# Recurrence of a streaming encoder layer: the chain of one tile placed among the levels of the next tile

## What is computed

```python
def wkv_scan(r, decay, k, v, kk, a, state0):
    def step(S, inp):
        r_t, w_t, k_t, v_t, kk_t, a_t = inp
        sa = jnp.einsum('bhij,bhj->bhi', S, -kk_t)
        S = (S * w_t[:, :, None, :] + sa[..., None] * (kk_t * a_t)[:, :, None, :]
             + v_t[..., None] * k_t[:, :, None, :])
        y = jnp.einsum('bhij,bhj->bhi', S, r_t)
        return S, y
...
    kk = kk * lax.rsqrt(jnp.maximum(jnp.sum(kk * kk, axis=-1, keepdims=True), 1e-24))
    k = k.astype(F32) * (1.0 + (a - 1.0) * k_a.astype(F32))
...
    y = ((y - mu) * lax.rsqrt(var + GN_EPS)).reshape(B, T, RWKV_WIDTH) * gn_g.astype(F32) + gn_b.astype(F32)
    y = y + (jnp.sum(r * k * r_k.astype(F32), axis=-1, keepdims=True) * v).reshape(B, T, RWKV_WIDTH)
    return y * jax.nn.silu(g.astype(F32)), S
```

## Time and profile before

| what | value |
| --- | --- |
| time, median of 3 runs (lowest, highest) | 1640.91 us (1640.88, 1646.04) |
| span of the profiled execution | 1640.3 us |
| PE busy | 1591.8 us (97%), 20218 matmuls |
| PEld busy | 1301.9 us (79%) |
| DVE busy | 806.8 us (49%) |
| ACT busy | 879.3 us (54%) |
| POOL busy | 498.8 us (30%) |
| gate matmuls, line 2529, gate_w_hi by gate_x_hi | 272 of them, 119.2 us, 438 ns each |

### The profile page before, as it was taken

The page is one execution under the profiler, slowest core; times in us unless marked ns, Lnnn a source line. Parts: engine busy times, 40 slices in busy tenths (PEclk is TensorE's granted clock), DMA queues, the critical chain, the costliest instruction groups (busy, mean ns, idle before and its releaser), DMA issues. The chain is left out here.

```text
span 1640.3 us, 46809 instructions
## 1 busy us (share of the span) xinstructions
PE 1591.8 (97%) x20218; PEld 1301.9 (79%) x20218; DVE 806.8 (49%) x1153; ACT 879.3 (54%) x1833; POOL 498.8 (30%) x354
## 2 busy tenths in 40 slices
PE   8999999999999899999998999999999997999999
PEld 7788888888888788899986777777777876777787
DVE  4344544454445531121226677667677677544432
ACT  6466566656665631222237777777777776224320
POOL 1423221222121012221223456455556456400000
PEclk9999999999999999999999999999999999999999
DMA  6323211122113543433353232232232236286652
GB/s 244 88 82 94 70 51 61 55 73 61 60 43 116 196 134 123 135 105 106 114 174 125 70 93 79 73 93 69 83 87 89 81 97 206 70 318 225 206 173 77
DMA packets 136302, 184.43 MB, mean 112 GB/s; under 512 B 59153, under 2 KB 88337, under 8 KB 135842
## 3 DMA queue, kind: packets, MB, share of 16 engines
q1 hardware_dynamic: 129186, 170.83, 32.3%
q10 hardware_dynamic: 6912, 10.62, 1.8%
HBM read 122.42 MB, written 59.55 MB: 111 GB/s over the span
## 5 line engine op out<-in xcount | busy, mean ns | idle before, releaser
L681 PE MATMUL a_ps_proj<-a_w_hi,a_x_hi 128*128 128x512 f32 x384 | 157.6, 410 | 2.5 <-ACT a_qk L431 1.4
L681 PE MATMUL a_ps_proj<-a_w_hi,a_x_lo 128*128 128x512 f32 x384 | 151.6, 395 | 0.0
L681 PE MATMUL a_ps_proj<-a_w_lo,a_x_hi 128*128 128x512 f32 x384 | 151.1, 393 | 0.0
L584 DVE SCALAR_TENSOR_TENSOR a_stage<-a_ps_s,a_new_bias 128x256 f32<-128x256 f32 x64 | 27.2, 425 | 241.5 <-PE a_ps_s L708 235.8
L2529 PE MATMUL r_ps_gate<-gate_w_hi,gate_x_hi 128*128 128x512 f32 x272 | 119.2, 438 | 5.2 <-PEq L66 3.4
L1187 DVE SCALAR_TENSOR_TENSOR j_out<-j_ps,j_rest,j_part 128x512 f32<-128x512 f32 (+2 forms) x45 | 29.0, 644 | 184.0 <-ACT j_last_cols L1131 139.1
L2529 PE MATMUL r_ps_gate<-gate_w_lo,gate_x_hi 128*128 128x512 f32 x272 | 111.6, 410 | 0.0
L360 POOL TENSOR_TENSOR a_xT<-a_xT,a_row 128x1024 f32<-128x1024 f32 x17 | 40.4, 2374 | 228.2 <-DMA a_row<-scratch_rstd 220.0
L469 ACT ACTIVATE a_stage<-a_stage,a_small 128x640 f32<-128x640 f32 (+4 forms) x128 | 95.8, 751 | 1.5 <-DVE a_small L592 1.5
L1061 POOL TENSOR_TENSOR j_v_prev<-j_v_prev,shift_x 128x512 f32<-128x512 f32 x17 | 22.2, 1307 | 228.3 <-DMA j_v_prev<-scratch_v_raw 216.7
L1129 ACT ACTIVATE j_part<-j_last_cols,j_shift_in 128x1 f32<-128x1 f32 x45 | 13.2, 294 | 141.7 <-PE j_ps L1220 141.7
(11 more groups left out here) (414 smaller groups left out, 4677.6 us busy)
## 6 DMA issues: line engine op xcount, KB each, us to landing
a_xT<-in_x_T SPq DMA_DIRECT2D x17, 512.0 KB, 3.4
scratch_xT<-a_xT SPq DMA_DIRECT2D x17, 512.0 KB, 2.6
raw<-scratch_xT SPq DMA_DIRECT2D x17, 512.0 KB, 4.8
scratch_gates<-r_gate_out SPq DMA_DIRECT2D x34, 256.0 KB, 2.4
z_gate<-scratch_gates SPq DMA_DIRECT2D x17, 512.0 KB, 4.6
a_x<-in_x_prompt SPq DMA_DIRECT2D x16, 512.0 KB, 3.6
o_x<-in_x_prompt SPq DMA_DIRECT2D x14, 512.0 KB, 4.9
out_y_prompt<-o_y SPq DMA_DIRECT2D x14, 512.0 KB, 2.9
```

Source lines behind the costliest of these rows:

```text
L584: nc.vector.scalar_tensor_tensor(out=out[:, :, OLD:WIN], in0=ps_new, scalar=SCALE, in1=new_bias[:, 2 * c:2 * c + 2, :], op0=ALU.mult, op1= ...
L681: mm = nc.tensor.matmul(ps_proj[:], a[n % 2][:, k, :], w[:, k, g * AW:(g + 1) * AW], start=(k == 0 and i == 0), stop=(k == KT - 1 and i == 2))
```

## The change

The part `back` is split in two, `levels` and `chain`, and in the pass of tile t stands the chain of tile t-1, sorted by its own numbers among the levels of t, with the tail of t-1 behind it:

```diff
-        def tiles(eng, front, back, mix=nothing, tail=nothing, gates=nothing, first_gates=nothing, out=nothing):
+        def tiles(eng, front, levels, chain=nothing, mix=nothing, tail=nothing, gates=nothing, first_gates=nothing, out=nothing):
...
-                run = [back(t, u, mode_of(t))]
+                run = [levels(t, u, mode_of(t))]
                 if t > 0:
-                    run.append(tail(t - 1, 1 - u, "p"))
+                    run += [chain(t - 1, 1 - u, "p"), tail(t - 1, 1 - u, "p")]
                 if t < DEC:
                     run.append(front(t + 1, 1 - u, mode_of(t + 1)))
                 else:
-                    run.append(later(tail(DEC, u, "s"), LAST_TAIL))
+                    run += [chain(DEC, u, "s"), later(tail(DEC, u, "s"), LAST_TAIL)]
```

The pass of tile 0 has no chain, and the pass of tile 16 has two, those of 15 and 16. The solve's results move into the second job bank, and the numbers change; the levels are 3.0 apart:

```diff
-        JOB_ORDER = ((("bonus", -1), ("decay", 0), ("k_tok", -1), ("B0", -1), ("B1", -1)),
-                     (("iclr", 0), ("b_tok", -1), ("K0", -1), ("K1", -1), ("kk_sum", 0)))
+        JOB_ORDER = ((("bonus", -1), ("k_tok", -1), ("B0", -1), ("B1", -1), ("decay", 0)),
+                     (("u0", -3), ("u1", -3), ("b_tok", -1), ("K0", -1), ("K1", -1), ("iclr", 0), ("kk_sum", 0)))
+        LAST_OF = {"u0": DEC - 2, "u1": DEC - 2}
...
-        LEVEL_AT, CHAIN_AT = 4.1, (20.5, 26.85)
-        GRAM_AT = (25.05, 28.15)
+        LEVEL_AT, Q_AT, CHAIN_AT = 3.0, 1.4, (20.5, 26.85)
+        GRAM_AT = (13.6, 15.5)
...
-        GATE_BLOCKS = (((1.1, 5), (3.2, 5), (5.2, 5), (7.3, 5), (9.3, 4)), ((13.4, 4), (17.5, 4), (19.6, 4), (23.6, 4), (28.9, 8)))
+        GATE_BLOCKS = (((2, 5), (4.6, 5), (8, 5), (12.3, 5), (14.5, 4)), ((16.6, 10), (18.5, 14)))
```

The 48 gate matmuls of a tile stand in seven blocks, before in ten. The chain of a prompt tile on PE, cut:

```diff
+                yield 0.2
+                wait(pe, state_ready, 2 * t)
+                wait(pe, ready["y_centred"], t)
...
+                    value(t, u, 1, 0, c, ps_y, c == 0)
+                    last = from_state(0, 0, ps_rhs, c, False, c == PAIRS - 1)
+                last.then_inc(rhs_written, 1)
...
+                yield 1.6
+                pe.wait_ge(rhs_ready, 2 * t + 1)
+                pe.wait_ge(z_ready, LP * t + L)
+                done = solved(0)
+                for c in range(PAIRS):
+                    value(t, u, 1, 1, c, ps_y, False)
+                    last = solve(0, c)
+                last.then_inc(done, 1)
+                yield 3.2
...
+                    value(t, u, 0, 1, c, ps_rhs, c == 0)
+                    last = to_state(0, c)
+                last.then_inc(s_written, 1)
+                yield 3.5
+                read_out(0)
```

More of the change, by code:

```diff
@@ L1694, in back @@
                                      states[:, :, now, :].rearrange("p c b d -> p c (b d)")).then_inc(stored, 16)
-            tiles(sp, front, back, mix, tail, gates, first_gates, out)
+            tiles(sp, front, nothing, chain, mix, tail, gates, first_gates, out)
             for j in range(2):
@@ L1826, in out @@
                     split_out_w(k)
-            tiles(pool, front, back, mix, tail, gates, out=out)
+            tiles(pool, front, nothing, chain, mix, tail, gates, out=out)
         @block.scalar
@@ L2037, in out @@
                     act.dma_start(rows_of(io["y_prompt"], D)[P:2 * P, OUT_X[j]], gate_out[j][:]).then_inc(y_stored[j], 16)
-            tiles(act, front, back, mix, tail, gates, first_gates, out)
+            tiles(act, front, levels, chain, mix, tail, gates, first_gates, out)
         @block.vector
@@ L2137, in decay_state, with levels @@
                                         ALU.mult).then_inc(state_ready, 1)
-            def back(t, u, mode):
+            def levels(t, u, mode):
                 L = LEVELS[mode]
@@ L2284, in out @@
                 add_x(1, 0)
-            tiles(dve, front, back, mix, tail, gates, first_gates, out)
+            tiles(dve, front, levels, chain, mix, tail, gates, first_gates, out)
             add_x(1, 1)
@@ new lines, in chain @@
+                yield 7.6
+                pe.wait_ge(rhs_ready, 2 * t + 2)
+                done = solved(1)
+                for c in range(PAIRS):
+                    first_values(t + 1, 1 - u, c)
+                    last = solve(1, c)
+                last.then_inc(done, 1)
+                yield 9.2
+                was_read(pe, t, "u1")
+                for c in range(PAIRS):
+                    last = to_state(1, c)
+                last.then_inc(s_written, 1)
+                yield 9.5
@@ L2600, in out @@
                     products(b // 12, b // 6 % 2, b % 6)
-            tiles(pe, front, back, mix, gates=gates, first_gates=first_gates, out=out)
+            tiles(pe, front, levels, chain, mix, gates=gates, first_gates=first_gates, out=out)
 def output_phase(nc, io, shared):
```

375 lines of the change are left out of this document (195 added, 180 removed).

## The result

The changed kernel takes 1738.86 us, median of 4 runs (1730.85 to 1739.13), beside 1643.47 us for the kernel before (1640.88 to 1646.07): a ratio of 1.057, 95% interval 1.055 to 1.060. The forecast was 1673.7, with a range from 1642 to 1698. The direction was right; the loss of 95 us is nearly three times the 32.8 forecast, and outside the range.

The account below looks back on a forecast made before the run. The prediction took a lora-ACT-solve-PE circle as the bound: 32.0 us plus 1.4 of DVE waits makes 33.4 a pass, +37.8 over 14 passes, +32.8 with the ends, so 1673.7 us; range 1642 to 1698.

Parts of the forecast that it names:

- PE's work: PE's dense pass: three gate blocks fewer save 0.84 us, chain groups add 0.47, giving about 29.5 us.
- The key sums wait a little themselves, but what they lose ends before ACT does and costs nothing on its own.: PE at the key sums, between lora products and solve: a small wait, priced at nothing beside ACT's 8.8 us.
- The ACT circle: Lora products, ACT to `r_rhs` (8.8 us), solve, PE back (23.2): at least 32.0 us a pass, PE waiting 2.6 at solve.
- DVE ahead of level 4 and at the grams: PE waits 1.1 us for level 4's mask and 0.3 between the two chunks' grams: 1.4 us a pass.
- the 0.57 that I called idle: PE's idle time a pass in the kernel before, (429.6 - 421.6) / 14 us: all the order could still win there.
- The clock falls: Rival: PE's wait at the solve lowers the clock each pass, 1.7 us added, +24, 1697 us; chance 0.08.
- The ends: Outside the steady passes: first pass -2.7 us, ahead of it -2, tile 15's pass -4.3, last pass +4.

Follow-up runs that it names:

- the kernel with the mix in the middle: Changed kernel with lora products ahead of W of level 3, sigmoids behind them, scan ahead of the second masks, ACT's table loads between other steps: 1682.9 us.
- Splitting the blocks: Changed kernel with its last two gate blocks of 6 and 18 matmuls instead of 10 and 14, lora products four matmuls earlier: 1735.5 us.
- putting the sigmoids first: Changed kernel with last gate blocks of 6 and 18, and ACT's sigmoids ahead of the crossed copy: 1719.2 us.
- the scan came first: Kernel with blocks of 6 and 18 and sigmoids ahead of the crossed copy, plus DVE's scan ahead of `z_mat` and POOL's square behind it: 1740.4 us.
- moving the copy: Against the kernel with DVE's scan ahead of `z_mat`: ACT's right-hand-side copy goes ahead of the table load and exponentials; 1718.8 us.
- the extra matmuls: Changed kernel with twelve more gate matmuls in the block of 14 ahead of the key sums, gates wrong: 1735.3 us.
- fine blocks: Kernel with the mix in mid-pass, its 48 gate matmuls in eleven blocks instead of seven, ACT's first gate copy moved earlier: 1743.5 us.

## Why the prediction was wrong

Per steady pass I forecast 33.4 us: 29.5 of work and 3.9 of waiting. Measured: 36.7, of which 5.45 is waiting and 31.2 work. Split by the kernel with the mix in the middle, the work is some 30.0 at the upper clock and 1.2 for the clock.

- *PE's work.* 29.5 was 0.5 too low. A gate block costs 0.22 and not 0.28, which takes 0.2 off the saving; the rest isn't placed.
- *"The key sums wait a little themselves, but what they lose ends before ACT does and costs nothing on its own."* This is the step that failed. PE stands there for 3.02 us, and at the solve not at all over the 11 passes. I followed the sigmoids from the lora products and did not ask what stood ahead of them on ACT: the crossed copy, at the end of masks, identity and `z_mat` of the second grams. In the kernel before that row of steps ended far from the key sums; the change put the grams, the mix and the key sums one behind the other. Splitting the blocks (wait 3.05, no gain) and putting the sigmoids first (wait 1.97, 16 us less) show it. The forecast also priced DVE's rows as in the kernel before. With `z_mat` and the low part at their old 0.69 us each the wait would be some 1.2 us, my estimate (3.02 - 1.8); no run took this apart. By size alone the error was small, 3.0 against 2.6, and that nearness is chance: the wait is another one.
- *The ACT circle* was real. It lay just behind the one that bound, and took over with 1.84 us when the scan came first; moving the copy then gave 21.6 us. In the changed kernel it cost nothing.
- *DVE ahead of level 4 and at the grams*, 1.4 forecast: 0.46 and 0.31. The places were right and the sizes too high; no run took this apart.
- *Stalls without a releaser* were not in the sum at all; before, they were most of the 0.57 that I called idle. They are 1.65 a pass, 1.3 more than before, and so the second largest part of the waiting. This term was put at nothing without a reason.
- *"The clock falls"* had chance 0.08 and was costed at 1.7 us a pass. It fell in 12 of 14 passes, for 1.2 a pass. I set the wait against the work between, "2.6 us in 9", though the one row that I had the earlier trace rows showed a single wait of 2.46 us followed by 6 us at the lower clock. That row deserved more than the argument against it. The section HAM oscillation of the Trainium skill's TensorE: Matmul & The Clock Gate describes an array that slows down anew at each wait between bursts of matmuls, and the trace agrees in those 12 passes: 3.0 us of waiting, then the clock at 0.50. But the work was not time: 1.0 us of it was won back with the extra matmuls, and the pass got 0.3 shorter. My +24 for this rival took work for time.
- *The ends.* First pass -2.7 forecast, +1.8 measured; start -2 and +1.4; tile 15 -4.3 and -1.9; last pass +4 and +9.8, at the upper bound. Together 16 us too low. No experiment took these apart. The trace shows PE standing 6.1 us at the first key sums ahead of the first pass, and in the last pass 2.8 us for the gate `z_gate` of the output, 2.1 at masks and 1.6 for `r_rhs`.

The differences in a steady pass, +0.5 work, +1.2 clock, +0.4 at the key sums against the solve, +1.65 stalls, less 0.6 at DVE, make some 3.2, or 45 of the 64 us by which the span's growth passed the forecast; most of the rest are the ends. The range reached 1698 because I let the cases exclude each other. The wait and the clock came together: with the wait filled the clock stayed up.

## What to carry to other kernels

Before costing a wait from the instruction that feeds it, read the row ahead of that instruction on its own engine: in a static order the thing ahead in the queue can start the chain instead of the data. When work is pulled into an already dense order, sum the rivals that bring each other (a wait, the slower clock behind it), and test each term by a kernel before believing it: an edit worth nothing in one order was worth 21.6 us in the next. Look up how long an instruction takes beside its new neighbours too, not only where it stands. And fillers are not spare work: the gate blocks covered masks and, ahead of the key sums, could hold the clock; and stalls without a releaser were rare where packets fell among them.

## What the runs showed of the hardware

PE's stalls that no semaphore explains go with its instruction packets: 202 of 224 end 0.7 to 2.2 us ahead of the start of one. They come most where a packet falls 80 or more narrow records after the last wide matmul (12 of 24 with the change, 6 of 12 before, 1 of 2 with fine blocks), hardly ever within wide ones (1 of 23), and reach 2.5 us. The Trainium skill, Runtime: NRT & Kernel Launch, section Instruction fetch mechanics, says that instruction fetch is hidden, since the sequencer issues more slowly than the fetch fills. The stalls beside the packets, 1.65 us a pass with the change, speak against that in stretches of 64x64 products; no run shows that the fetch is what PE waits for.

DVE's low part, `kk_lo`, took 0.69 us in the kernel before, 0.88 with the scan first, 0.78 with the mix in the middle, and 1.68 with the change in 10 of 11 passes (1.33 in one), the same instruction on data of the same shape. The row of the kernel before:

```profile
1246.36 0.69 DVE L2074 TENSOR_TENSOR r_kk_lo<-r_sig,r_kk_hi 128x512 fp32r<-128x512 f32 x1 [1.89 <-ACT r_kk_hi L1837]
```

What makes the difference can be read from POOL's timeline. Before, POOL is idle beside it. In the changed kernel it starts while POOL is at an instruction of the tail, and ends after that one has ended and the next has begun:

```profile
1246.14 1.27 POOL L1798 TENSOR_TENSOR r_y_tok<-r_y_tok,params 128x512 f32<-128x512 f32 x1
1247.48 1.60 POOL L1801 TENSOR_TENSOR r_y_tok<-r_y_tok,r_y_sq 128x512 f32<-128x512 f32 x1
```

The low part ends at 1247.95, 0.47 us into the second. With the mix in the middle and with the scan first it also ends 0.47 us into the next POOL instruction, but has stood beside only 0.23 and 0.34 us of the one before. `z_mat` does the same in the changed kernel, 1.52 us beside two POOL instructions of the tail instead of 0.69 beside none, and again 0.47 us into the second. So in these four cases the DVE instruction takes longer by what the POOL instruction under way still has to run, less some 0.15 us. No run moved the tail alone, so what the two cost in time is not measured.
